# RWKV scan: the 64-by-64 triangular inverse as two 32-by-32 diagonal blocks and a corner product

## What is computed

```
def step(S, inp):
    r_t, w_t, k_t, v_t, kk_t, a_t = inp
    sa = jnp.einsum('bhvk,bhk->bhv', S, -kk_t)
    S = (S * w_t[:, :, None, :] + sa[..., None] * (kk_t * a_t)[:, :, None, :]
         + v_t[..., None] * k_t[:, :, None, :])
    return S, jnp.einsum('bhvk,bhk->bhv', S, r_t)
...
_, y = lax.scan(step, S0, (tm(r_h), tm(w_h), tm(k_h), tm(v_h), tm(kk), tm(a_h)))
```

## Time and profile before

| | |
|---|---|
| median of three runs | 2615.81 us |
| profiled execution | 2612.05 us, its span 2610.3 us |
| mean granted TensorE clock | 0.981 |
| span of the scan's chunks, first output copy to last | 464.7 to 823.7 us, 15 chunks |
| TensorE matmuls / weight loads | 17850 / 17850 |
| VectorE / ScalarE / GpSimd instructions | 1787 / 1156 / 455 |

### The profile page before, as it was taken

The page is one execution under the profiler, slowest core; times in us unless marked ns, Lnnn a source line. Parts: engine busy times, 40 slices in busy tenths (PEclk is TensorE's granted clock), DMA queues, the critical chain, the costliest instruction groups (busy, mean ns, idle before and its releaser), DMA issues. The chain is left out here.

```text
span 2610.3 us, 42546 instructions
## 1 busy us (share of the span) xinstructions
PE 2453.6 (94%) x17850; PEld 1268.7 (49%) x17850; DVE 971.7 (37%) x1787; ACT 638.9 (24%) x1156; POOL 442.3 (17%) x455
## 2 busy tenths in 40 slices
PE   6999998888888989999999999998999799999998
PEld 3344444777776544343344344443945443334443
DVE  7335434677775352111111134215843611111114
ACT  4443001566664220000000121311633100000000
POOL 0022521344443001000001003121011100000000
PEclk8999999999999989999999999999999899999999
DMA  3334335333333437999999851261551789999997
GB/s 130 145 129 152 106 118 165 95 90 82 92 100 125 162 120 303 415 426 422 417 426 427 339 213 65 97 193 65 165 185 56 281 332 425 424 417 426 428 427 296
DMA packets 216552, 618.83 MB, mean 237 GB/s; under 512 B 40193, under 2 KB 157058, under 8 KB 189746
## 3 DMA queue, kind: packets, MB, share of 16 engines
q1 hardware_dynamic: 188946, 534.69, 53.5%
q10 hardware_dynamic: 14288, 48.25, 4.7%
q0 software_dynamic: 13136, 33.25, 3.2%
HBM read 540.96 MB, written 89.66 MB: 242 GB/s over the span
## 5 line engine op out<-in xcount | busy, mean ns | idle before, releaser
L2621 PE MATMUL moe_psum<-trunk_late,moe_x_t 128*64 128x512 f32 (+2 forms) x912 | 344.2, 593 | 0.9 <-DVE moe_x_t L2748 0.9
L2580 DVE TENSOR_TENSOR moe_buffers_both<-moe_buffers_both,moe_psum 128x512 f32<-128x512 f32 x46 | 49.9, 1085 | 625.2 <-ACT moe_buffers_both L2794 625.2
L2621 PE MATMUL moe_psum<-trunk_early,moe_x_t 128*64 128x512 f32 (+2 forms) x512 | 215.7, 602 | 2.5 <-ACT moe_x_t L2092 2.5
L2621 PEld LDWEIGHTS moe_psum<-trunk_late,moe_x_t 128*64 128x64 f32 (+2 forms) x912 | 121.4, 151 | 162.3 <-issue 161.2
L2636 POOL DMA_INDIRECT expert_rows<-moe_buffers_out,moe_scatter_row x45 | 45.7, 1016 | 869.6 <-DVE moe_buffers_out L2760 861.3
L2621 PE MATMUL moe_psum<-trunk_mixed,moe_x_t 128*64 128x512 f32 (+2 forms) x448 | 181.9, 593 | 0.0
L2794 ACT ACTIVATE moe_buffers_both<-moe_psum 128x512 f32<-128x512 f32 x46 | 27.5, 597 | 612.6 <-PE moe_psum L2621 612.6
L1934 PE MATMUL moe_psum<-trunk_late,trunk_mixed 128*128 128x512 f32 x384 | 170.4, 597 | 0.0
L2621 PE MATMUL moe_psum<-trunk_kept,moe_x_t 128*128 128x512 f32 (+2 forms) x368 | 147.9, 593 | 0.9 <-DVE moe_x_t L2748 0.9
L1445 ACT ACTIVATE scan_x<-scan_psum 64x256 f32<-64x256 f32 x320 | 121.2, 379 | 53.5 <-PE scan_psum L1519 29.5
L2621 PE MATMUL moe_psum<-trunk_late,moe_buffers_act_t 128*64 128x512 f32 (+2 forms) x304 | 134.2, 594 | 0.0
(11 more groups left out here) (522 smaller groups left out, 4419.8 us busy)
## 6 DMA issues: line engine op xcount, KB each, us to landing
trunk_late<-in_moe_w_in SPq DMA_DIRECT2D x49, 2048.0 KB, 19.7
trunk_early<-in_moe_w_in SPq DMA_DIRECT2D x28, 2048.0 KB, 20.4
trunk_mixed<-in_moe_w_in SPq DMA_DIRECT2D x22, 2048.0 KB, 21.8
trunk_kept<-in_moe_w_in SPq DMA_DIRECT2D x19, 2048.0 KB, 23.0
trunk_mixed<-in_moe_w_out SPq DMA_DIRECT2D x18, 2048.0 KB, 23.9
trunk_early<-in_moe_w_out SPq DMA_DIRECT2D x18, 2048.0 KB, 24.8
trunk_late<-in_moe_w_out SPq DMA_DIRECT2D x15, 2048.0 KB, 21.9
trunk_ninth<-in_moe_w_out SPq DMA_DIRECT2D x10, 2048.0 KB, 22.4
```

Source lines behind the costliest of these rows:

```text
L2580: return v.tensor_mul(self.act[:].rearrange("p (k q) -> p k q", k=FF // P), self.silu[:].rearrange(by_row, k=FF // P), self.value_p.rearra ...
L2621: mm = t.matmul(psum[rows, bank + a, :], left[:, k0 + k, rows], weights.units[unit.slot][:, k, a * HALF:(a + 1) * HALF], start=(part != "h ...
```

## The change

`LEVELS` becomes 4 and `SUB` = 32. The matrix I - X of each head is cut into two diagonal blocks of 32 by 32 and the corner between them. The diagonal blocks are inverted by five factors, with four squaring levels' matmuls of 32 rows by 32 columns of the array; the corner is then the product of the two inverses with X's corner. In the matmuls that the diff adds, `strip(...)` is a strip of 32 partitions, one for each head of a pair and block.

- Level 0: for each of the 4 strips of a pair a square, a transposed square and I+X (the product with `none_ident`'s identity), 12 matmuls a pair. Levels 1 to 3: 4 squares and 4 products a pair. `last_factors`: 4 a pair.
- New: `corner_sides` (4 a pair), a copy on VectorE (`turned_back`, step T), `corner` (6 a pair), a copy on VectorE (step Q).
- VectorE's copy and add of a level are one 128x256 addition (`factor`), to `lv`, whose first plane is zero. `add_identity` is gone from VectorE and from GpSimd. ScalarE's copies are 64x128.
- `risen` of the next trip moves from level 4 to level 3.

The core of the diff:

```diff
-LEVELS = 5
+LEVELS = 4
+SUB = 32
...
-        x = [s.sb(f"x{b}", [P, PAIRS, CHUNK]) for b in range(2)]
-        xp = [s.sb(f"xp{b}", [P, PAIRS, 2, CHUNK]) for b in range(2)]
+        x0 = s.sb("first_x", [P, PAIRS, CHUNK])
+        x = [s.sb(f"x{b}", [P, PAIRS, SUB]) for b in range(2)]
+        lv = [s.sb(f"lv{b}", [P, PAIRS, 3, SUB]) for b in range(2)]
+        none_ident = s.sb("none_ident", [P, 2, SUB])
+        inverse = s.sb("inverse", [P, PAIRS, CHUNK])
...
-        pe_steps += ["W.0"] + halves(f"XP{LEVELS}") + ["W.1"] + halves("U") + ["Y"] + halves("S")
+        pe_steps += ["W.0"] + halves(f"XP{LEVELS}", "T") + ["W.1"] + halves("Q", "U") + ["Y"] + halves("S")
...
-        def add_identity(engine, h, head):
-            return engine.tensor_tensor(xp[1][other[head], half[h], 1, :], kb_t[other[head], head, half[h], 0, :],
-                                        spread(c.ident_st[other[head], :], 1, PAIRS // 2), ALU.add)
+        def strip(heads, block):
+            return slice(heads.start + block * SUB, heads.start + (block + 1) * SUB)
+        def columns(block):
+            return slice(block * SUB, (block + 1) * SUB)
...
+                old, new = lv[j % 2], lv[(j + 1) % 2]
+                both = slim(XP_BANK + h).rearrange("p m (a e) -> p m a e", e=SUB)
+                if j == 0:
+                    start = spread(none_ident[:], 1, PAIRS // 2)
+                    return v.tensor_tensor(new[:, half[h], 1:3, :], both, start, ALU.add)
+                if j < LEVELS - 1:
+                    return v.tensor_tensor(new[:, half[h], 1:3, :], both, old[:, half[h], 0:3:2, :], ALU.add)
+                return v.tensor_tensor(new[:, half[h], 2, :], both[:, :, 1, :], old[:, half[h], 2, :], ALU.add)
+            def turned_back(h):
+                sides = psum[:, 2 * h:2 * h + 2, 0:PAIRS // 2 * SUB].rearrange("p n (m e) -> p m n e", e=SUB)
+                v.tensor_copy(lv[0][:, half[h], 1:3, :], sides).then_inc(dve.sem, 1)
+            def corner(h):
+                v.tensor_copy(inverse[:, half[h], :], slim(X_BANK + h)).then_inc(dve.sem, 1)
...
-                            if j < LEVELS - 1:
-                                v.tensor_copy(xp[(j + 1) % 2][:, half[h], 0, :],
-                                              wide(XP_BANK + h)[:, :, 0:CHUNK]).then_inc(dve.sem, 1)
-                            if j:
-                                v.tensor_add(xp[(j + 1) % 2][:, half[h], 1, :], xp[j % 2][:, half[h], 1, :],
-                                             wide(XP_BANK + h)[:, :, CHUNK:P]).then_inc(dve.sem, 1)
+                            if chunk == 0 and j == 0 and h == 0:
+                                v.wait_ge(ready, READY)
+                            factor(j, h).then_inc(dve.sem, 1)
...
-                        if j == 4 and b == 1 and not last:
+                        if j == 3 and b == 1 and not last:
                             risen(trip + 1, 0, "K")
                             risen(trip + 1, 0, "B")
+                    for h in range(2):
+                        v.wait_ge(pe.sem, pe.after(f"T.{h}", chunk))
+                        turned_back(h)
+                    for h in range(2):
+                        v.wait_ge(pe.sem, pe.after(f"Q.{h}", chunk))
+                        corner(h)
...
-                                back = a.activation(x[j % 2][other[head], half[h], :], slim(X_BANK + h)[own[head]], ACT.Copy)
+                                back = a.activation(x[j % 2][other[head], half[h], :], thin(X_BANK + h)[own[head]], ACT.Copy)
...
+            def squares(h, j):
+                old, last_old = lv[j % 2], half[h].stop - 1
                 for m in range(half[h].start, half[h].stop):
                     at = m - half[h].start
...
+                    for head, block in BLOCKS:
+                        src, to = strip(other[head], block), strip(own[head], block)
+                        if j == 0:
+                            left, right = kb_t[src, head, m, 0, columns(block)], x0[src, m, columns(block)]
+                        else:
+                            left, right = old[src, m, 1, :], x[j % 2][src, m, :]
+                        square = t.matmul(thin(X_BANK + h)[to, at, :], left, right, start=True, stop=True)
+                    if m == last_old:
                         square.then_inc(pe.sem, 1)
...
+                    for head, block in BLOCKS:
+                        src = strip(other[head], block)
+                        out = slim(XP_BANK + h)[src, at, :]
+                        if j == 0:
+                            left, right = x0[src, m, columns(block)], kb_t[src, head, m, 0, columns(block)]
+                            t.matmul(out[:, columns(0)], left, right, start=True, stop=True)
+                            factor = t.matmul(out[:, columns(1)], left, none_ident[src, 1, :], start=True, stop=True)
+                        elif j < LEVELS - 1:
+                            both = old[src, m, 1:3, :].rearrange("p a t -> p (a t)")
+                            factor = t.matmul(out, x[j % 2][src, m, :], both, start=True, stop=True)
+                        else:
+                            factor = t.matmul(out[:, columns(1)], x[j % 2][src, m, :], old[src, m, 2, :],
+                                              start=True, stop=True)
                 factor.then_inc(pe.sem, 1)
...
+            def last_factors(h):
+                for m in range(half[h].start, half[h].stop):
+                    for head, block in BLOCKS:
+                        src = strip(other[head], block)
+                        mm = t.matmul(slim(XP_BANK + h)[src, m - half[h].start, columns(1)], x[LEVELS % 2][src, m, :],
+                                      lv[LEVELS % 2][src, m, 2, :], start=True, stop=True)
+                mm.then_inc(pe.sem, 1)
+            def corner_sides(h):
+                for m in range(half[h].start, half[h].stop):
+                    at = m - half[h].start
+                    for head in range(2):
+                        upper, lower = strip(other[head], 0), strip(other[head], 1)
+                        t.matmul(thin(2 * h + 1)[upper, at, :], lv[1][upper, m, 2, :], none_ident[upper, 1, :],
+                                 start=True, stop=True)
+                        mm = t.matmul(thin(2 * h)[upper, at, :], x0[lower, m, columns(0)],
+                                      lv[1][lower, m, 2, :], start=True, stop=True)
+                mm.then_inc(pe.sem, 1)
+            def corner(h):
                 for m in range(half[h].start, half[h].stop):
                     for head in range(2):
...
+                        upper, lower = strip(other[head], 0), strip(other[head], 1)
+                        out = slim(X_BANK + h)[:, m - half[h].start, :]
+                        t.matmul(out[upper, columns(0)], none_ident[upper, 1, :], lv[1][upper, m, 2, :], start=True, stop=True)
+                        t.matmul(out[lower], none_ident[lower, 1, :], lv[1][lower, m, 0:3:2, :], start=True, stop=True)
+                        mm = t.matmul(out[upper, columns(1)], lv[0][upper, m, 2, :], lv[0][upper, m, 1, :],
+                                      start=True, stop=True)
+                mm.then_inc(pe.sem, 1)
...
-                            t.wait_ge(act.sem, act.after(f"X{j}.{h}", chunk))
-                            if j == 1 and h == 1:
-                                t.wait_ge(second_factor, 2 * chunk + 2)
+                                if chunk == 0 and h == 0:
+                                    t.wait_ge(ready, READY)
                             else:
+                                t.wait_ge(act.sem, act.after(f"X{j}.{h}", chunk))
                                 t.wait_ge(dve.sem, dve.after(f"P{j - 1}.{h}", chunk))
-                            t.wait_ge(dve.sem, dve.after(f"XT{j}.{h}", chunk))
-                            squares(h, x[old], xp[old], slice(0, P) if j < LEVELS - 1 else slice(CHUNK, P))
+                            squares(h, j)
...
-                        row = last_factors(h, b, a_b, last_x, last_pt)
-                    row.then_inc(pe.sem, 1)
-                    inverse = xp[(LEVELS + 1) % 2][:, :, 1, :]
+                        last_factors(h)
+                    t.wait_ge(dve.sem, dve.after(f"P{LEVELS}.0", chunk))
+                    corner_sides(0)
+                    t.wait_ge(dve.sem, dve.after(f"P{LEVELS}.1", chunk))
+                    corner_sides(1)
+                    wanted(1, b, a_b)
+                    for h in range(2):
+                        t.wait_ge(dve.sem, dve.after(f"T.{h}", chunk))
+                        corner(h)
                     for h in range(2):
                         t.wait_ge(act.sem, act.after(f"W.{h}", chunk))
-                        t.wait_ge(dve.sem, dve.after(f"P{LEVELS}.{h}", chunk))
-                        each_head(slim(XP_BANK + h), half[h], inverse, w_st)
+                        t.wait_ge(dve.sem, dve.after(f"Q.{h}", chunk))
+                        solved(h)
```

(62 more changed lines are left out.)

33 lines of the change are left out of this document (7 added, 26 removed).

## The result

| | before | after |
|---|---|---|
| median of four runs | 2614.88 us | 2799.52 us |
| profiled execution, its span | 2612.05, 2610.3 us | 2799.52, 2797.8 us |
| scan, first output copy to last (15 chunks) | 464.71 to 823.73 us | 475.15 to 1007.33 us |
| one chunk | 23.93 us | 35.48 us |

After to before is 1.0706, 95% interval 1.0683 to 1.0729: 185 us slower, where 160 were forecast. The 15 chunks of the scan grew from 359.0 to 532.2 us, 173.2; with the sixteenth, 173.2 x 16/15 = 184.7 us, so the scan holds all of it.

What follows compares the result with a forecast made beforehand. TensorE's instruction fetch was taken to bound the scan: 32.0 us for 8.5 blocks plus 2 us for loads, 34.0 a chunk against 24.0, so 160 us over 16 chunks and 2776 us in all; range 2705 to 2832.

Steps and rivals of the forecast that it cites:

- The count of instructions: TensorE in the scan: 896 more instructions a chunk, 2176 in place of 1280, 8.5 fetch blocks in place of 5.0.
- The 3.77 us a block: TensorE's instruction fetch in the scan: mean time per block of 256 instructions, giving 32.0 us a chunk for 8.5 blocks.
- the prediction's sign of being wrong: In the profile after: instruction packets closer than 3.3 us, or stalls ending at semaphores rather than at "issue".
- second rival: In the scan, fetch keeps up and TensorE's stream decides: +0.5 us a chunk, 2624 us; chance 0.04.
- third rival: In the scan's levels, small parts run side by side and copies bound: 2.4 us a chunk saved, 2578 us; chance 0.03.
- what comes on top of the floor: Scan blocks lengthened by loads ahead of a fetch, 2 us a chunk; blocks' own longer work was given nothing.
- The loads: Data loads standing in front of instruction fetches in the scan: 2 us a chunk beyond the measured mean.
- Saved work of VectorE and ScalarE: In the scan, VectorE falls from 8.7 to 5.8 us a chunk and ScalarE's copies shrink; no time gained beside the fetch.
- Stalls over 100 us in all: Sign in the scan after: many idle stretches of TensorE's loads before "issue", together over 100 us.
- The granted clock: TensorE's clock falling below today's 0.97 to 0.99: only a reason to round the high end from 2827 to 2832.
- fourth rival: Level 0's repeated stationary operand isn't loaded twice: 15 us less in all, 2761; a variant within the fetch-bound 0.93.
- The forecast's own doubt: About the fetch bound in the scan: only a few intervals clean, none showing many saturated blocks in a row.

Runs made afterwards that it cites:

- e8_after_noloads: Kernel after the change, with the scan's input loads after the first trip replaced by semaphore counts: 2776.09 us, ratio 1.0626.
- e6_after_copies: Kernel after the change, with each of ScalarE's copies of the powers made twice, first into an unread buffer: 2794.21 us, ratio 1.0696.
- e4_wide: Kernel after the change, plus an unread matmul of 256 columns on the whole array ahead of each half-level: 2803.78 us, ratio 1.0734.
- e3_fewer: Kernel after the change, with the corner's identity products replaced by one masked VectorE multiplication for each half: 2794.05 us, ratio 1.0703.
- e10_before_bf16: Kernel before the change, with powers and partial products of the squarings in bfloat16: 2604.79 us, ratio 0.9966.

## Why the prediction held, point by point

- The count of instructions was right: 896 more a chunk (894 with the waits), 196 packets, 8.53 blocks a chunk.
- The 3.77 us a block, read from three pairs of stalls, hold as a typical value: the 82 stalled blocks after have a median of 3.78 us, a mean of 3.90, and 3.71 without the loads. As a floor they were read too high. The prediction said that no block comes faster than every 3.6 us or so, and packets 3.6 to 4.2 us apart nearly throughout; of the 127 distances between the starts of q8's packets after, 32 are under 3.6 us, 50 in that range and 45 above. Closer than 3.3 us, the prediction's sign of being wrong, is one of them, at 3.25. That a block can be asked for only in the one before it, where the earlier trace rows had shown it, held under pressure: 125 of the 127 blocks after hold the start of one packet, 1.24 us (median) from their beginning where they stall. The second and the third rival needed the opposite.
- Against the rule of the Trainium skill (Runtime: NRT & Kernel Launch, section on instruction fetch mechanics) that fetch is hidden behind the sequencer's issue, the gaps at every 256th record speak, 142.7 us in 15 chunks; the stalled blocks after had run for 2.2 us on average when they began to wait for the next one.
- The term that was mis-sized is what comes on top of the floor: 2.0 us forecast, 3.3 measured. By the table of blocks, 8.53 x 3.77 = 32.2; stalled blocks above the floor 82 x (3.90 - 3.77)/15 = 0.7; blocks longer by their own work 45 x (4.61 - 3.77)/15 = 2.5; together 35.4 of the measured 35.48. The prediction put nothing for the last ("I add nothing more and leave them to the range"), on the thought that most waits hide. They don't: a third of the blocks doesn't stall, and of these most run longer than the floor for their own work and waits. In e8_after_noloads the same sum, at its 3.71 us for a stalled block, is 31.6 + 44 x (4.56 - 3.71)/15 = 34.1 of 34.16, so the long blocks are not the loads' doing. The loads were taken at 2 and cost 1.3, and the two errors partly cancel: 1.5 us by 16 is 24 of the 25 us between 160 and 185.
- Saved work of VectorE and ScalarE brought nothing, as said; ScalarE's narrower copies took 272 ns, between the bounds of 190 and 379, and the value taken was the upper one, which cost nothing, since e6_after_copies shows the engine off the path.
- Stalls over 100 us in all: 155. Chunks of 34 us: 35.5.
- The granted clock was only let into the high end, by 5 us. It fell to 0.78, further than thought; e4_wide, with 0.91, took no less time. Its own share of the 2.8 us of longer running was not isolated.
- The fourth rival (repeated weights not loaded) is out: 25018 loads to 25018 matmuls. The forecast's own doubt, that many saturated blocks in a row had not been seen, is answered by 82 of 127. The second rival's stream was about as long as it said (3.3 us a chunk there, 2.8 of longer running measured); what it left out is the gaps.

## What to carry to other kernels

In unrolled code count TensorE's instructions (a float32 matmul is four, a bfloat16 one two) and look for waits on "issue" 256 instructions apart. In this scan each added instruction cost 12 to 15 ns, running and fetch together (894 for 11.6 us a chunk, 880 for 12.7, 440 for 6.0), and the smaller tiles of the array lost, since they needed more matmuls. The helpers' smaller copies gave nothing back, and the 128 instructions that e3_fewer took out brought next to nothing. Doubling a suspected copy told the two bounds apart in one run each. Adding instructions that do nothing did not by its total, since they take time to run as well; summing the gaps at every 256th record did.

## What was not expected of the hardware

- The granted clock fell from 0.99 to 0.78 in the scan. From 688.00 to 691.80 us it was 1.00; in 691.80 to 695.70, nearly all of it a stall, 0.71; and the next stretch, 695.70 to 699.54, ran at 0.50, the 1.2 GHz level. The sums of the group norm took 998 ns a matmul where they had taken 618. That gaps from instruction fetch are the only reason is not shown: e10_before_bf16 has hardly any and its clock was 0.85.
- In the 15 chunks of all 14 kernels that ran, no two packets of q8 start less than 3.2 us apart, though in the kernel after TensorE had done with a stalled block's 256 instructions after 2.2 us on average.
- The same count of instructions gave the same time within 0.2%, 29.88 and 29.94 us a chunk, with 1-column matmuls between large ones and with 32-by-32 parts, out of different shares of running, stalls and waits.
- Matmuls of one column are no cheaper in the end: 880 instructions of them cost 12.7 us a chunk, 14.5 ns each, a little over the real work's 12.9, though a burst of 88 runs at 6.1 ns each.
